# POOL makes the low parts of the weights in pieces of 256 columns in place of 512

## The chip, the cores and the metric

The kernel runs on one core of one Trainium2 chip. The time is the device time of one execution in microseconds (us). The engines are named as the profile names them: PE (matrix multiplications), PEld (its weight loads), ACT, DVE and POOL (elementwise work), SP (issues transfers). Each engine runs its own instruction stream, and the streams wait for each other by semaphores.

## The reference

Two transformer-like layers over x of 512 tokens by 1024 features, all in float32. Layer 0 mixes by a gated linear recurrence (4 heads) beside a differential attention (4 heads), layer 1 by an attention with forget gates (16 heads); each layer ends in a SwiGLU block.

```python
def reference(x, even_w_in, even_w_out, ..., fox_w_in, fox_w_out, ..., ffn_w1, ffn_w2, ln1_g, ln1_b, ln2_g, ln2_b):
    for l in range(DEPTH):          # DEPTH = 2, D_MODEL = 1024, SEQ = 512, D_FF = 2816
        j = l // 2
        if l % 2 == 0:
            h = _even_mixer(x, even_w_in[j], even_w_out[j], lb_all[j], ..., l)
        else:
            h = _odd_mixer(x, fox_w_in[j], fox_w_out[j], fox_b_f[j], fox_qnorm_g[j], fox_knorm_g[j])
        x = _layer_norm(ALPHA * x + h, ln1_g[l], ln1_b[l])
        x = _layer_norm(ALPHA * x + _swiglu(x, ffn_w1[l], ffn_w2[l]), ln2_g[l], ln2_b[l])
    return x
```

Nearly all the arithmetic is products of x (or of an activation of the same height) with the weight matrices.

## The kernel before

**Split products.** Each float32 operand of a large product is split into a high part in PE's own format (fp32r) and a low part, the remainder. A product is then three matmuls, `high x low`, `low x high`, `high x high` (function `products`, lines 507 to 509), summed in a PSUM bank.

**Chunks of weights.** All weights are cut into 107 chunks in the order of use, nearly all of 2048 columns on 128 partitions (four have 1024, one has 128). A chunk passes four stations:

- SP loads it into `w_raw`, a ring of two (`load`, L1021). Before it loads chunk c it waits until the low part of chunk c-2 is made (`lo_ready`).
- ACT rounds it into `w_hi`, a ring of three, in one operation (`hi_upto`, L1118), at places in ACT's stream that are written out by hand. It waits for the load and for PE to be done with chunk c-3.
- POOL subtracts: `w_lo = w_raw - w_hi`, a ring of three (L1078), four operations of 512 columns a chunk. Only the last one reports (`lo_ready`). This is all that POOL does.
- PE waits for both parts (`weights_in`) before the first product with the chunk.

In the forgetting attention, POOL's operations of some chunks are each put behind a step of DVE (`lo_behind`: the operation waits for `qn_done`, the normalised queries and keys of one token tile, L1709), so that it runs in a stretch that DVE leaves free. The table has one entry for each 512 columns.

**Stages in order.** Input projections and the recurrence of layer 0 (0 to 190 us: PE alternates between pieces of projections and products of the recurrence, L811 to L834, while DVE scales `qT`, `kT`, `spans`, L1498 to L1501, and normalises heads, `refine`, L1440 to L1443, L1562); differential attention (190 to 285); output projection and layer norm (285 to 330; `norm`, L1633 to L1655, then `split_lo`, L1425); SwiGLU (330 to 690), layer norm; forgetting attention (695 to 997); output projection, layer norm, SwiGLU, layer norm (to 1401). In a layer norm, tile t of x passes through a fixed chain on DVE: L1633 adds the product to the residual, L1634 and L1641 take statistics, ACT forms a root, L1645 subtracts the mean and multiplies by the gain, L1648 to L1650 refine the root, L1655 scales and adds the bias. PE then turns the tile (L578), and ACT and DVE split it again.

The order of the instructions on each engine is fixed in the program. Nothing is planned at run time.

Of the kernel before, what the change touches and what calls it, by code (L numbers as in the profile page):

```python
# [128 lines left out]
def build(nc, w, out):  # L129
    chunks = weight_chunks(w)  # L130
    stage_chunks = {}
    for c, (stage, _, _) in enumerate(chunks):
        stage_chunks.setdefault(stage, []).append(c)

    with ExitStack() as ctx:
# [188 lines left out]
        n = 0  # L324
# [81 lines left out]
        for i, (piece, _) in enumerate(fox_steps):  # L406
            if piece:
                c, p = piece
                if c == chunk_at("foxk0") and p % 2 == 0:
                    round_at[i] = c + 1 + p // 2  # L410
                elif c != chunk_at("foxk0") and p == (3 if chunks[c][0] == "foxv0" else 1):
                    round_at[i] = c + 2
# [7 lines left out]
        def nth(kinds, u):  # L420

            return sum(1 for k, _, _ in units[:u] if k in kinds)
# [644 lines left out]
        @block.gpsimd  # L1067
        def _(pool):
            for c, (_, _, size) in enumerate(chunks):
                pool.wait_ge(hi_ready, c + 1)  # L1070
                if c >= RING:
                    pool.wait_ge(*chunk_used[c - RING])
                for a in range(0, size, 512):
                    n = min(512, size - a)
                    behind = lo_behind.get(c, [None] * 4)[a // 512]
                    if behind:
                        pool.wait_ge(S["qn_done"], behind)
                    ins = nc.gpsimd.tensor_tensor(w_lo[c % RING][:, a:a + n], w_raw[c % RAW][:, a:a + n],  # L1078
                                                  w_hi[c % RING][:, a:a + n].bitcast(F32), ALU.subtract)
                ins.then_inc(lo_ready, 1)  # L1080
# [780 lines left out]
```

## Time and profile before

| | |
|---|---|
| time, median of 3 runs | 1402.65 us (1400.98 to 1405.59) |
| the profiled execution's own time | 1402.81 us |
| its span, first to last instruction | 1401.0 us |
| PE busy | 1348.9 us, 96% |
| DVE busy | 474.6 us, 34% |
| ACT busy | 495.6 us, 35% |
| POOL busy | 531.5 us, 38%, 417 operations of L1078 |
| mean granted clock of PE | 0.989 of 2.4 GHz |

The span is the profiler's view of the execution. 1.8 us of the device time lie outside it. Ends of PE's matmuls are modelled and overlap, so that their spacing, not their duration, tells what one costs.

### The profile page before, as it was taken

The page shows a single profiled execution, that of the slowest core. Times are in us where ns is not written, and L with a number is a line of the kernel's source. Part 1 is how long each engine was busy: PE and PEld are TensorE (multiplying, and loading weights), DVE is VectorE, ACT ScalarE, POOL GpSimd, SP SyncE. Part 2 cuts the span into 40 slices and gives each one's busy share as a digit, 9 for nine tenths or more (in the row PEclk, how much of TensorE's full clock was granted, in tenths as well). Part 3 has the DMA queues.
Part 4 walks back from the last instruction along what each step waited for, and adds up shares of the span by engine and source line. Part 5 has one row for each costly group of instructions (what it writes and reads, how often), then busy time and mean ns, then how long its engine had stood idle before and what let it go on. Part 6 is the DMA issues. An engine that isn't in the chain of part 4 may idle for free.

```text
span 1401.0 us, 18949 instructions
## 1 busy us (share of the span) xinstructions
PE 1348.9 (96%) x7304; PEld 1125.0 (80%) x7304; DVE 474.6 (34%) x956; ACT 495.6 (35%) x824; POOL 531.5 (38%) x421
## 2 busy tenths in 40 slices
PE   7998999698999999999999999999999999999997
PEld 7887877588888888888788888877788888888886
DVE  3365435556111111010634555644561111110005
ACT  4313155523322232211255665654333222232111
POOL 5514041232444445544234312222434444445440
PEclk9999999799999999999999999999999999999999
DMA  6311021113333332333133222211223333323221
GB/s 213 110 61 61 31 92 60 61 33 89 91 91 90 104 107 76 120 97 127 25 96 94 66 62 61 61 61 61 91 85 96 90 90 95 108 84 120 91 105 60
DMA packets 141400, 119.60 MB, mean 85 GB/s; under 512 B 5664, under 2 KB 120576, under 8 KB 141312
## 3 DMA queue, kind: packets, MB, share of 16 engines
q1 hardware_dynamic: 141072, 118.10, 27.0%
q8 instruction: 58, 0.95, 0.3%
q10 hardware_dynamic: 240, 0.31, 0.1%
q14 instruction: 30, 0.25, 0.1%
HBM read 116.20 MB, written 2.10 MB: 84 GB/s over the span
## 4 chain that ended last, share of the span: by engine, by line
PE 83%; DVE 7%; ACT 4%; issue 4%; POOL 1%; DMA 0%; ACTq 0%; DVEq 0%; SPq 0%; POOLq 0%
PE banks L507 25%; PE banks L508 25%; PE banks L509 25%; ACT w_hi L1118 1%; PE banks L816 1%; PE banks L974 1%; PE banks L940 1%; PE banks L956 1%; POOL w_lo L1078 1%; PE banks L834 1%; DVE small L1602 1%; DVE xT_lo L1425 1%; PE banks L880 1%; DMA w_raw<-in_even_w_in_dram 0%; DVE x_res L1645 0%
## 5 line engine op out<-in xcount | busy, mean ns | idle before, releaser
L1078 POOL TENSOR_TENSOR w_lo<-w_raw,w_hi 128x512 fp32r<-128x512 f32 x417 | 531.3, 1304 | 838.1 <-ACT w_hi L1118 782.6
L507 PE MATMUL banks<-xT_lo,w_hi 128*128 128x512 f32 (+2 forms) x1024 | 384.3, 375 | 2.5 <-DVEq L1426 2.4
L509 PE MATMUL banks<-xT_hi,w_hi 128*128 128x512 f32 (+2 forms) x1024 | 380.5, 372 | 0.0
L508 PE MATMUL banks<-xT_hi,w_lo 128*128 128x512 f32 (+2 forms) x1024 | 380.4, 372 | 0.0
L1118 ACT ACTIVATE w_hi<-w_raw 128x2048 fp32r<-128x2048 f32 (+1 forms) x107 | 200.0, 1869 | 194.5 <-PE banks L509 151.4
L507 PEld LDWEIGHTS banks<-xT_lo,w_hi 128*128 128x128 f32 (+1 forms) x1024 | 192.2, 188 | 37.4 <-issue 5.1
L509 PEld LDWEIGHTS banks<-xT_hi,w_hi 128*128 128x128 f32 (+1 forms) x1024 | 192.1, 188 | 33.6
L508 PEld LDWEIGHTS banks<-xT_hi,w_lo 128*128 128x128 f32 (+1 forms) x1024 | 192.2, 188 | 32.6
L1675 DVE TENSOR_TENSOR banks<-silu_g,banks 128x512 f32<-128x512 f32 x44 | 30.6, 696 | 403.1 <-PE banks L509 403.1
L507 PE MATMUL banks<-w_lo,xT_hi 128*128 128x256 f32 (+1 forms) x480 | 159.0, 331 | 5.1 <-POOL w_lo L1078 2.8
L508 PE MATMUL banks<-w_hi,xT_lo 128*128 128x256 f32 (+1 forms) x480 | 153.9, 321 | 0.0
L509 PE MATMUL banks<-w_hi,xT_hi 128*128 128x256 f32 (+1 forms) x480 | 153.8, 320 | 0.0
L507 PE MATMUL banks<-w_lo,hT_hi 128*128 128x512 f32 x352 | 137.1, 390 | 0.0
L509 PE MATMUL banks<-w_hi,hT_hi 128*128 128x512 f32 x352 | 137.0, 389 | 0.0
L508 PE MATMUL banks<-w_hi,hT_lo 128*128 128x512 f32 x352 | 136.9, 389 | 0.0
L1288 ACT ACTIVATE silu_g<-banks 128x512 f32<-128x512 f32 x44 | 26.3, 597 | 306.9 <-PE banks L509 306.9
L507 PEld LDWEIGHTS banks<-w_lo,xT_hi 128*128 128x128 f32 x480 | 92.1, 192 | 15.2 <-issue 6.5
L509 PEld LDWEIGHTS banks<-w_hi,xT_hi 128*128 128x128 f32 x480 | 92.2, 192 | 6.6
L508 PEld LDWEIGHTS banks<-w_hi,xT_lo 128*128 128x128 f32 x480 | 92.4, 192 | 5.9
L1633 DVE SCALAR_TENSOR_TENSOR x_res<-x_res,banks 128x512 f32<-128x512 f32 x32 | 22.0, 687 | 212.5 <-PE banks L509 211.8
L509 PEld LDWEIGHTS banks<-w_hi,hT_hi 128*128 128x128 f32 x352 | 66.1, 188 | 13.7
L507 PEld LDWEIGHTS banks<-w_lo,hT_hi 128*128 128x128 f32 x352 | 66.1, 188 | 13.7
(198 smaller groups left out, 1259.9 us busy)
## 6 DMA issues: line engine op xcount, KB each, us to landing
w_raw<-in_ffn_w_dram SPq DMA_DIRECT2D x92, 512.0 KB, 4.6
w_raw<-in_ffn_w_dram SPq DMA_DIRECT2D x20, 1024.0 KB, 4.9
w_raw<-in_fox_w_in_dram SPq DMA_DIRECT2D x16, 1024.0 KB, 5.8
w_raw<-in_even_w_in_dram SPq DMA_DIRECT2D x14, 1024.0 KB, 5.0
w_raw<-in_even_w_out_dram SPq DMA_DIRECT2D x4, 1024.0 KB, 5.1
w_raw<-in_fox_w_out_dram SPq DMA_DIRECT2D x4, 1024.0 KB, 5.0
x_res<-in_x_dram SPq DMA_DIRECT2D x4, 512.0 KB, 7.9
out_dram<-x_res SPq DMA_DIRECT2D x3, 512.0 KB, 2.6
```

The costliest lines, as they stand in the source:

```text
L507: mm(acc, l_hi, r_lo, start=first, stop=False)
L508: mm(acc, l_lo, r_hi, start=False, stop=False)
L509: return mm(acc, l_hi, r_hi, start=False, stop=final)
L816: ins = mm(halves(acc[:, tok], z)[:, :, 1, :], k[:, tok], halves(q[:, tok], z)[:, :, 1, :], start=True, stop=True)
L834: ins = mm(acc[:, t * P:(t + 1) * P], scT[:, h % 2, PAIR[(s, t)], :], iv[:, s, h * P:(h + 1) * P], start=s == 0, stop=s == t)
L880: mm(acc[:, 0:n], bqT[rows, h, i * P:(i + 1) * P], bkT[rows, h, 0:n], start=True, stop=False)
L940: mm(acc[:, 0:n], qk[rows, j % 2, 0, pair % 2, i * P:(i + 1) * P], qk[rows, j % 2, 1, pair % 2, 0:n], start=True, stop=False)
L1078: ins = nc.gpsimd.tensor_tensor(w_lo[c % RING][:, a:a + n], w_raw[c % RAW][:, a:a + n], w_hi[c % RING][:, a:a + n].bitcast(F32), ALU.subtract)
L1118: chain(fn(w_hi[c % RING][:, 0:size], w_raw[c % RAW][:, 0:size], ACT.Copy), hi_ready)
L1288: release(fn(silu_buf(j), acc[:, :], ACT.Silu), (f"up{l}", j, 0))
L1633: release(stt(xs, xs, ALPHA, full(key)[:, :], ALU.mult, ALU.add), key)
L1675: release(tt(h_buf(j), silu_buf(j), acc[:, :], ALU.mult), (f"up{l}", j, 1))
```

## The change

POOL's loop steps by 256 columns and not by 512. A chunk of 2048 columns takes eight operations in place of four, one of 1024 takes four in place of two, and the one of 128 columns stays one operation. The data, the ring buffers, the semaphore and the place where it is raised (after the last operation) are the same. The entry of `lo_behind` is still taken by 512 columns, so two operations in a row wait for the same value, of which the second wait is met at once.

```
--- before.py
+++ after.py
@@ -1070,8 +1070,8 @@
                 pool.wait_ge(hi_ready, c + 1)
                 if c >= RING:
                     pool.wait_ge(*chunk_used[c - RING])
-                for a in range(0, size, 512):
-                    n = min(512, size - a)
+                for a in range(0, size, 256):
+                    n = min(256, size - a)
                     behind = lo_behind.get(c, [None] * 4)[a // 512]
                     if behind:
                         pool.wait_ge(S["qn_done"], behind)
```

## Rows read from the trace of the kernel before

**Rows 1.** The page, part 1: busy time and share of each engine.

```profile
PE 1348.9 (96%) x7304; PEld 1125.0 (80%) x7304; DVE 474.6 (34%) x956; ACT 495.6 (35%) x824; POOL 531.5 (38%) x421
```

**Rows 2.** The waits: who waited for whom, us in total, times, longest.

```profile
POOL w_lo L1078 <- ACT w_hi L1118: 782.6, 103, 33.9
...
PE banks L816 <- DVE spans L1501: 7.0, 6, 3.3
PE banks L890 <- ACT pT_diff L1246: 4.3, 3, 2.1
...
PE banks L507 <- POOL w_lo L1078: 2.8, 2, 2.4
...
PE banks L507 <- issue: 2.2, 2, 1.8
```

**Rows 3.** The timeline of POOL in the first SwiGLU: start, duration, operation, idle before.

```profile
395.30 5.04 POOL L1078 TENSOR_TENSOR w_lo<-w_raw,w_hi 128x512 fp32r<-128x512 f32 x4 [5.84 <-ACT w_hi L1118]
```

**Rows 4.** The timelines of POOL and DVE at 310 and at 695 us.

```profile
310.06 2.34 POOL L1078 TENSOR_TENSOR w_lo<-w_raw,w_hi 128x512 fp32r<-128x512 f32 x1
309.96 1.29 DVE L1645 SCALAR_TENSOR_TENSOR x_res<-x_res,stats,rows_even 128x1024 f32<-128x1024 f32 x1
...
313.89 1.29 DVE L1655 SCALAR_TENSOR_TENSOR x_res<-x_res,stats,rows_even 128x1024 f32<-128x1024 f32 x1
...
696.42 1.44 POOL L1078 TENSOR_TENSOR w_lo<-w_raw,w_hi 128x128 fp32r<-128x128 f32 x1
695.19 2.36 DVE L1645 SCALAR_TENSOR_TENSOR x_res<-x_res,stats,rows_ffn 128x1024 f32<-128x1024 f32 x1
...
698.11 0.16 DVE L1650 SCALAR_TENSOR_TENSOR stats<-stats 128x1 f32<-128x1 f32 x1
```

**Rows 5.** The timeline of POOL at the start: its four smallest operations.

```profile
0.24 0.10 POOL L1850 MEMSET const-float32-0.0<- 128x1 f32 x1 [0.24 <-issue]
...
0.34 0.10 POOL L1850 MEMSET const-uint8-127<- 128x1 uint8 x1
```

**Rows 6.** The timelines of POOL, DVE and PE in the opening.

```profile
10.46 4.97 POOL L1078 TENSOR_TENSOR w_lo<-w_raw,w_hi 128x512 fp32r<-128x512 f32 x4 [10.02 <-ACT w_hi L1118]
14.77 0.69 DVE L1425 TENSOR_TENSOR xT_lo<-banks,xT_hi 128x512 fp32r<-128x512 f32 x1 [0.22 <-DVE xT_lo L1425]
15.53 0.36 PE L507 MATMUL banks<-xT_lo,w_hi 128*128 128x256 f32 x1 [0.63 <-DVEq L1426]
```

**Rows 7.** The timelines of POOL and PE where the forgetting attention starts.

```profile
691.49 6.37 POOL L1078 TENSOR_TENSOR w_lo<-w_raw,w_hi 128x512 fp32r<-128x512 f32 x5 [23.25 <-ACT w_hi L1118]
696.72 0.36 PE L507 MATMUL banks<-w_lo,xT_hi 128*128 128x256 f32 x1 [2.39 <-POOL w_lo L1078]
```

**Rows 8.** The timelines of POOL and PE at the second output projection.

```profile
997.71 10.02 POOL L1078 TENSOR_TENSOR w_lo<-w_raw,w_hi 128x512 fp32r<-128x512 f32 x8 [28.55 <-ACT w_hi L1118]
1007.88 0.47 PE L507 MATMUL banks<-w_lo,xT_hi 128*128 128x512 f32 x1 [0.45 <-POOL w_lo L1078]
1029.69 0.55 PE L578 MATMUL banks<-ident,x_res 128*128 128x128 f32 x3 [0.74 <-DVE x_res L1655]
```

**Rows 9.** The timelines of POOL and PE at two chunks of the forgetting attention.

```profile
716.72 1.26 POOL L1078 TENSOR_TENSOR w_lo<-w_raw,w_hi 128x512 fp32r<-128x512 f32 x1 [2.13 <-DVE qn L1709]
718.08 0.36 PE L507 MATMUL banks<-w_lo,xT_hi 128*128 128x256 f32 x1 [1.79 <-issue]
729.69 1.29 POOL L1078 TENSOR_TENSOR w_lo<-w_raw,w_hi 128x512 fp32r<-128x512 f32 x1 [0.95 <-DVE qn L1709]
731.08 0.47 PE L507 MATMUL banks<-w_lo,xT_hi 128*128 128x512 f32 x1 [0.39 <-issue]
```

**Rows 10.** The timelines of POOL, DVE and PE in the recurrence.

```profile
135.09 4.99 POOL L1078 TENSOR_TENSOR w_lo<-w_raw,w_hi 128x512 fp32r<-128x512 f32 x4 [4.50 <-ACT w_hi L1118]
136.42 1.22 DVE L1441 TENSOR_TENSOR stats<-stats 128x4 f32<-128x4 f32 x1
138.92 1.19 DVE L1443 TENSOR_TENSOR stats<-stats 128x4 f32<-128x4 f32 x1
140.14 1.25 DVE L1562 TENSOR_SCALAR o_even<-o_even,stats 128x128 f32<-128x128 f32 x4
142.47 0.74 PE L816 MATMUL banks<-qT,kT 128*128 128x64 f32 x5 [3.27 <-DVE spans L1501]
```

**Rows 11.** Windows: busy us (x instructions) of PE, PEld, DVE, ACT, POOL, then PE's clock.

```profile
697.00:701.00 4.00, 4.00 (x23) 4.00 (x22) 3.61 (x7) 0.04 (x1) 0.86 (x1) 0.57 0.84 226
701.00:706.00 5.00, 5.00 (x45) 4.80 (x45) 0.78 (x2) 1.20 (x2) 0.00 (x0) 1.00 0.64 242
```

More of the change, by code:

```diff
@@ L1072, in _ @@
                     pool.wait_ge(*chunk_used[c - RING])
-                for a in range(0, size, 512):
-                    n = min(512, size - a)
+                for a in range(0, size, 256):
+                    n = min(256, size - a)
                     behind = lo_behind.get(c, [None] * 4)[a // 512]
```

## The prediction

> **What bounds the kernel now.** The page's busy times come first: PE is busy 96% of the span, POOL 38% [rows 1]. PE sets the end, and POOL is no bound by its sum. The waits come second: POOL stood idle 782.6 us for ACT's high parts, and PE waited for POOL only twice, 2.8 us in all [rows 2]. In the SwiGLU stages, half the span, a chunk takes POOL 5.04 us and then it idles 5.84 us [rows 3]; a longer batch there disappears in that idle time. So the change can act in two ways only. It can delay the few chunks for whose low part PE stands waiting, or it can change how POOL and DVE get in each other's way. The third look was therefore at each of PE's idle gaps in the timeline, and at each operation of DVE that took longer beside POOL than its like did elsewhere.
>
> **POOL and DVE take turns.** At 309.96 DVE's L1645 and POOL's third operation start together. DVE takes its usual 1.29 us, to 311.25; POOL takes 2.34, to 312.40, 1.15 us after DVE [rows 4]. The other way round, L1441 and L1443 work on 4 columns and take 1.22 and 1.19 us [rows 10], where a DVE operation of that size with no POOL beside it takes 0.16 [rows 4]; each ends with the POOL operation that runs beside it. So a POOL operation and a DVE operation that reads two SBUF tensors exclude each other, and one that waits gets its turn when the other ends.
>
> **The price of one operation.** Two POOL operations of different width were held up by DVE: the 512 columns ended 1.15 us after it, the 128 columns at 697.86, 0.31 us after DVE's 697.55 [rows 4]. That is 0.84 us for 384 columns, 2.19 ns a column, or 1.12 us for 512 and 0.56 for 256. Four operations of 512 take 5.04 us, of which the last lasts 1.29, so they follow each other every 1.25 us [rows 3]. The rest, 1.25 - 1.12 = 0.13 us, is what an operation costs whatever its width. One of 256 then follows every 0.69 us, and a chunk takes 8 x 0.69 + 0.04 = 5.56 us for 5.04, 0.52 more. The fixed 0.13 us is the disputed number. From below, the smallest POOL operations follow each other every 0.03 us [rows 5]; from above, the whole 0.31 us of the 128 columns may be fixed [rows 4]. I take 0.13, because it follows from the very operation that is cut. In sum POOL gains 416 operations, 54 us, nearly all of it in its idle time.
>
> The Trainium skill (GPSIMD Engine Reference, section Elementwise, side-by-side cycle accounting) gives 2.6 cycles an element at 1.2 GHz for this operation, 2.17 ns, and 4497 ns for 2048 elements, which leaves 0.06 us fixed. The trace agrees on the slope. By the page's 0.06 the sum below would come to about +1.5 us.
>
> **Part by part, on PE's path.**
>
> *Opening.* POOL makes the first chunk's low part from 10.46 to 15.43; DVE's last needed split ends at 15.46; PE starts at 15.53 [rows 6]. Both are due together, so POOL's 0.52 us go onto the path: +0.5.
>
> *Start of the forgetting attention.* POOL works from 691.49; its fifth operation, which belongs to the next chunk, starts at 696.42, so the fourth ends at 696.46, and PE, idle since 694.33, starts at 696.72 [rows 7]. DVE's L1645 was issued at 695.19, just missed its turn, and ended at 697.55, 1.09 after POOL's last operation [rows 4]. With operations every 0.69 us, the sixth runs from 694.94 to 695.67 when L1645 is issued. L1645 gets the next turn, ends at 696.76, and two POOL operations are still to come: the first ends 0.31 + 128 x 0.00219 = 0.59 after it, the second 0.69 later, at 698.04. PE starts 1.6 us later, at 698.3. DVE gains nothing by it, since L1648 to L1650 now each wait for one of POOL's left operations. +1.6.
>
> *Second output projection.* Two chunks in a row, 8 operations, 10.02 us; PE waits 0.45 us for the end [rows 8]. Sixteen take 11.08: +1.06. PE later waits for DVE's layer norm by 0.74 us [rows 8], and that chain moves by somewhat less. +0.8.
>
> *Two chunks of the forgetting attention.* POOL's last quarter, put behind DVE's L1709, ends at 717.98 and 730.98, and PE starts 0.10 us after each; the waits call these 1.79 and 0.39 us "issue" [rows 2, 9]. Each quarter is now two operations: +0.13 twice, +0.3.
>
> *DVE's delays.* Where DVE runs several such operations in a row, halving POOL's does not halve the delay. After 136.1 POOL had three operations of 1.25 us to go, and L1441 to L1443 waited for one each; the four L1562 behind them then ran free in 1.25 us [rows 10]. Now six or seven of 0.69 us are to go: L1440 to L1443 wait some 0.5 us each, and three of the L1562 wait 0.4 to 0.5 each. Played through turn by turn, the row ends at 141.2 to 141.4 for 141.4 before. The chain at 309.96 ends at 315.18 (313.89 + 1.29) both times [rows 4]: L1645 and L1648 to L1655 wait for the four halves that the two whole ones were. What POOL still has to do when DVE arrives passes between DVE's operations in either cut. Only where DVE turns to PSUM or idles after one or two operations does something come back; I count -0.4 for the recurrence.
>
> Sum: 0.5 + 1.6 + 0.8 + 0.3 - 0.4 = +2.8 us. On the profiled execution, 1402.8, that is 1405.6; its own time lies 0.16 above the median, so against 1402.65 the forecast is 1405.4. The loads cost nothing: SP starts the next one 0.5 us later, and a chunk that is rounded every 10.9 us (5.04 + 5.84) hides it [rows 3]; without that cover it would be 0.5 us a chunk.
>
> **Rivals.**
>
> *DVE gets half its waits back (faster).* Nine of POOL's batches run shortly ahead of a gap of PE, and in each about two operations of DVE wait 1.05 us (1.22 - 0.17): 19 us. If short operations let DVE pass after half the time and no further waits came in, 9.5 would come back, less 3.2 of costs: 1396. For it speaks that each wait is a whole POOL operation long [rows 10]; against it the turn-by-turn count above, and that PE waits for ACT's copies (4.3 us, L1246) in the differential attention beside its 7.0 us for DVE's `spans` [rows 2]. It decides from some 7.4 us given back. The Trainium skill (SBUF — State Buffer, section Who interferes with whom) says that the one issued first holds the shared ports for the whole instruction and the other fully blocks; by that rule alone, shorter holds free DVE sooner. The trace agrees with the rule.
>
> *An operation costs more than 0.13 us fixed (slower).* 4 + 4 + 8 + 2 = 18 extra operations lie on PE's path. At the bound of 0.31 they cost 5.6 for 2.3 us: +6.1, 1408.8. It decides from about 0.21.
>
> *PE's clock (slower).* After the 2.4 us gap before 696.72 the granted clock fell: 0.57 on average from 697 to 701, 1.00 after [rows 11]; 23 matmuls ran in 4 us there against 45 in 5 us. A gap of 4 us may be followed by a longer stretch at 1.2 GHz, or a second place may fall. One such stretch costs 4 - 23/9 = 1.4 us; two more make +5.6, 1408.2.
>
> *No effect at all:* 1402.7, if the fixed cost is the 0.03 and DVE does not get in at 695.
>
> **How the numbers follow.** This measurement tells no change from one of 0.3%, 4.2 us. Forecast 0.60, inside that; no effect 0.05, inside; DVE's waits come back 0.08, of which 0.07 beyond; fixed cost 0.15 and clock 0.12, beyond. So faster 0.07, same 0.66, slower 0.27. The range reaches from 1401.5 (bound of 0.03, and a little given back) to 1410 (the two slower rivals, partly together). The forecast's own range is 1404 to 1406.8.
>
> **What would show it.** POOL: 833 operations of L1078, median near 0.73 us, 5.56 us for eight in the SwiGLU. PE's first L507 at 16.0; its gap at 694.3 near 4 us, with L1645 there at 1.57 us, not 2.36; its gap at 1007.4 near 1.5. The gap at 139.2 about as long as before. Eight operations in well over 5.8 us would make the fixed cost wrong; a gap at 694 that stayed at 2.9 would mean that DVE did not get in between; clearly shorter gaps of PE at 127 to 142 would show DVE's waits coming back.

## The result: 3.5 us slower, where 2.8 us was forecast

The kernel with 256 columns takes 1406.49 us (median of 14 runs, 1405.43 to 1408.77), the one before, beside it on the same chip, 1402.94 us (14 runs). The ratio is 1.0029, with a 95% interval of 1.002 to 1.0038. Against the 1402.65 us that the forecast was made on, +3.55 us is 1406.2; the forecast was 1405.4 with a range of 1401.5 to 1410. The profiled execution has a span of 1404.3 us for 1401.0, and a mean granted clock of 0.986 for 0.989.

Part 1 of the page after, and POOL's group (operations | busy us, mean ns of one | idle us, and for whom). They answer to [rows 1]:

```profile
PE 1351.9 (96%) x7304; PEld 1127.6 (80%) x7304; DVE 467.3 (33%) x956; ACT 496.3 (35%) x824; POOL 595.2 (42%) x837
...
L1078 POOL TENSOR_TENSOR w_lo<-w_raw,w_hi 128x256 fp32r<-128x256 f32 x833 | 595.0, 751 | 778.0 <-ACT w_hi L1118 727.0
```

POOL works 63.7 us more (54 were predicted), and its wait for ACT is 55.6 us shorter (782.6 in [rows 2]): the extra work lies in its idle time. DVE is busy for 7.3 us less, which is waiting that no longer sits inside its operations. PE is busy for 3.0 us more with the same 7304 matmuls; that goes with more time at the lower clock (worked out from the two traces: 42.5 us of the span at a granted clock of 0.50, before 33.4).

The timeline of POOL after, at the four places of [rows 6, 3, 7, 8]:

```profile
10.49 5.54 POOL L1078 TENSOR_TENSOR w_lo<-w_raw,w_hi 128x256 fp32r<-128x256 f32 x8 [10.05 <-ACT w_hi L1118]
...
395.84 5.61 POOL L1078 TENSOR_TENSOR w_lo<-w_raw,w_hi 128x256 fp32r<-128x256 f32 x8 [5.27 <-ACT w_hi L1118]
...
692.03 6.95 POOL L1078 TENSOR_TENSOR w_lo<-w_raw,w_hi 128x256 fp32r<-128x256 f32 x9 [22.98 <-ACT w_hi L1118]
...
999.76 11.16 POOL L1078 TENSOR_TENSOR w_lo<-w_raw,w_hi 128x256 fp32r<-128x256 f32 x16 [27.96 <-ACT w_hi L1118]
```

A chunk costs 5.54 to 5.61 us for a predicted 5.56, two in a row 11.16 for 11.08. In the SwiGLU the idle before it shrinks from 5.84 to 5.27 us and nothing else moves.

The timeline of PE after, where it waits (answers to [rows 6 to 9]):

```profile
16.13 0.36 PE L507 MATMUL banks<-xT_lo,w_hi 128*128 128x256 f32 x1 [0.98 <-POOL w_lo L1078]
...
698.82 0.55 PE L507 MATMUL banks<-w_lo,xT_hi 128*128 128x256 f32 x1 [3.95 <-POOL w_lo L1078]
...
720.10 0.35 PE L507 MATMUL banks<-w_lo,xT_hi 128*128 128x256 f32 x1 [1.94 <-issue]
...
733.25 0.47 PE L507 MATMUL banks<-w_lo,xT_hi 128*128 128x512 f32 x1 [0.56 <-issue]
...
1011.07 0.47 PE L507 MATMUL banks<-w_lo,xT_hi 128*128 128x512 f32 x1 [1.61 <-POOL w_lo L1078]
...
1032.92 1.09 PE L578 MATMUL banks<-ident,x_res 128*128 128x128 f32 x8 [0.75 <-DVE x_res L1655]
```

The wait of 2.39 us became 3.95, those of 1.79, 0.39 and 0.45 us became 1.94, 0.56 and 1.61. The last row is the later wait for DVE's layer norm: 0.75 for 0.74 us, so nothing of the longer wait at 1007 us is given back there.

PE issues the same matmuls in the same order in both kernels, so the start of the same matmul can be compared. Worked out from the two traces, us:

```
PE's matmul no.        32     500    724    760    1250   1650   3330   3560   5490   5600   7300
start before           15.53  98.24  142.47 150.15 242.74 338.09 702.37 733.00 1003.2 1027.9 1392.2
after minus before     +0.59  +0.37  +0.64  -1.33  -1.50  +0.54  +1.87  +2.17  +2.04  +3.21  +3.31
```

From 338 us on, every step of more than 0.15 us in this row is one of the predicted waits. Before 338 us the kernel gains 2 us at 144 and loses them again between 250 and 335. That is what the forecast did not have, and what half of the experiments are about.

### The profile page after: what moved, and what is told of

It is laid out like the page before. It is cut to its first block, busy times and chain, and to the rows that moved or that the text cites. A ratio compares the mean times of both kernels' runs of the same rounds, so it can differ in the third digit from the quotient of the medians.

```text
span 1404.3 us, 19365 instructions
## 1 busy us (share of the span) xinstructions
PE 1351.9 (96%) x7304; PEld 1127.6 (80%) x7304; DVE 467.3 (33%) x956; ACT 496.3 (35%) x824; POOL 595.2 (42%) x837
## 4 chain that ended last, share of the span: by engine, by line
PE 84%; DVE 6%; ACT 4%; issue 4%; POOL 2%; DMA 0%; ACTq 0%; DVEq 0%; SPq 0%; POOLq 0%
PE banks L507 25%; PE banks L509 25%; PE banks L508 25%; POOL w_lo L1078 2%; PE banks L816 2%; ACT w_hi L1118 1%; PE banks L974 1%; PE banks L940 1%; PE banks L956 1%; PE banks L834 1%; PE banks L578 1%; PE banks L880 1%; DMA w_raw<-in_even_w_in_dram 0%; DVE x_res L1645 0%; DVE small L1602 0%
## 5 line engine op out<-in xcount | busy, mean ns | idle before, releaser
L1078 POOL TENSOR_TENSOR w_lo<-w_raw,w_hi 128x256 fp32r<-128x256 f32 x833 | 595.0, 751 | 778.0 <-ACT w_hi L1118 727.0
L508 PEld LDWEIGHTS banks<-w_hi,hT_lo 128*128 128x128 f32 x352 | 66.1, 188 | 13.6
```

Source lines behind the costliest of these rows:

```text
L508: mm(acc, l_lo, r_hi, start=False, stop=False)
```

## Where the clock was low

The granted clock is 1.00 at 2.4 GHz and 0.50 at 1.2 GHz. The windows of PE before and after (busy us and number of instructions of PE, PEld, DVE, ACT, POOL; then PE's granted clock, DMA share, GB/s), first of the kernel before:

```profile
135.09:141.92 6.83, 3.86 (x20) 3.07 (x20) 6.37 (x12) 0.00 (x0) 4.99 (x4) 1.00 0.09 20
144.26:147.67 3.41, 3.41 (x13) 2.97 (x12) 2.65 (x9) 0.00 (x0) 0.00 (x0) 0.50 0.06 17
```

and of the kernel after:

```profile
135.09:141.92 6.83, 4.77 (x15) 4.19 (x16) 6.37 (x13) 0.00 (x0) 5.25 (x8) 0.50 0.16 45
144.11:147.67 3.56, 3.43 (x20) 3.02 (x20) 3.02 (x9) 0.00 (x0) 0.00 (x0) 1.00 0.15 50
...
698.29:701.71 3.42, 2.89 (x13) 2.92 (x14) 3.10 (x5) 0.00 (x0) 0.69 (x2) 0.50 0.53 114
```

Before, PE ran at 1.2 GHz from 144.26 us, when it was busy without a gap: 13 matmuls in 3.41 us, where after it does 20 in 3.56. After, it runs at 1.2 GHz from 135.09 to 141.92 us. In that stretch it would have waited for DVE's `spans` anyway, 3.27 us before 142.47 [rows 10]. Twice as long at the lower clock cost nothing that was left at matmul 732, and once at the wrong moment cost 1.6 us (matmuls 732 to 760).

The timelines of PE and DVE after, in this stretch, and behind them one row of DVE before (they answer to [rows 10]):

```profile
133.76 1.08 PE L816 MATMUL banks<-qT,kT 128*128 128x64 f32 x8 [2.22 <-DVE spans L1501]
137.15 1.94 PE L816 MATMUL banks<-qT,kT 128*128 128x64 f32 x8 [2.31 <-DVE spans L1501]
...
143.11 2.21 PE L816 MATMUL banks<-qT,kT 128*128 128x64 f32 x16
...
134.53 0.87 DVE L1498 TENSOR_TENSOR qT<-qT,spans 128x256 f32<-128x256 f32 x1
135.33 0.94 DVE L1499 TENSOR_TENSOR kT<-kT,spans 128x256 f32<-128x256 f32 x1
136.19 0.81 DVE L1501 TENSOR_TENSOR spans<-spans 128x128 f32<-128x128 f32 x1
...
137.91 0.38 DVE L1440 TENSOR_TENSOR stats<-stats 128x4 f32<-128x4 f32 x1
138.33 0.65 DVE L1441 TENSOR_TENSOR stats<-stats 128x4 f32<-128x4 f32 x1
139.01 0.66 DVE L1442 TENSOR_SCALAR stats<-stats 128x4 f32<-128x4 f32 x1
139.71 0.65 DVE L1443 TENSOR_TENSOR stats<-stats 128x4 f32<-128x4 f32 x1
...
141.69 0.42 DVE L1498 TENSOR_TENSOR qT<-qT,spans 128x256 f32<-128x256 f32 x1
```

```profile
141.43 0.43 DVE L1498 TENSOR_TENSOR qT<-qT,spans 128x256 f32<-128x256 f32 x1
```

Each DVE wait is halved (0.65 - 0.17 = 0.48 us for 1.05), and there are twice as many: POOL's batch starts at 134.40 and not at 135.09, and L1498 to L1501 wait 0.44, 0.52 and 0.53 us beside the three at L1441 to L1443. With L1440 that is 3.15 us of waiting for 3.23 before. DVE starts the L1498 behind its row 0.26 us later than before (141.69 for 141.43); it had started the L1498 ahead of the row 0.30 us later (134.53 for 134.23). So DVE's chain is as long as it was, to 0.04 us.

PE has no gap at matmul 724 any more, since the matmuls ahead of it are slow enough to fill it. It starts this matmul at 143.11 us, 0.64 later than before and 0.38 later than `spans` would have let it (ready at 142.58, and before at 142.32 for a start at 142.47). Eight matmuls on it waits for DVE's next `spans` again, 0.13 us, and is 0.26 us late. What is gained comes afterwards, from the clock: 1.6 us up to matmul 760.

## The experiments

Theory A is the forecast's: the cost stands at six chunks (first of all, `foxq0`, `foxk0`, `foxv0`, and the two of the second output projection), and is POOL's time there plus one turn lost to DVE. The rivals stand beside it in each expectation. The widths are set at the two changed lines; `piece` is the number of columns of one operation, and `chunk_at` gives a chunk's number. "Beside" names the kernel before as it ran on the same chip. Its median differs from one such series to the next (1402.14 to 1404.5 us), so that ratios are compared and not times. A trace shows one execution of a kernel, and a kernel with one run has no interval.

**1 and 2. The six chunks alone at 512, and alone at 256.**

```diff
-                for a in range(0, size, 256):
-                    n = min(256, size - a)
+                for a in range(0, size, piece := 512 if c in CRITICAL else 256):    # kernel 1
+                for a in range(0, size, piece := 256 if c in CRITICAL else 512):    # kernel 2
+                    n = min(piece, size - a)
```

`CRITICAL` stands for the numbers of `a_f` 0, `foxq0`, `foxk0`, `foxv0` 0 and `out1` 2 and 3.

> Pieces of 256 everywhere, but of 512 in the six chunks for whose low part PE stood waiting (the first of a_f, foxq0, foxk0, the first of foxv0, the last two of out1). Theory A (the time is lost at those six chunks, by the fixed cost of the extra operations and by DVE's turn at 695): PE's gaps there are those of the kernel before (0.6, 2.4, 1.8, 0.4 and 0.5 us) and the time is back at 1402 to 1403.5. Theory B (the loss is spread over the other 101 chunks, by port traffic, semaphores or the clock): no more than 1 us comes back, 1405.5 to 1406.5.

> The complement: pieces of 256 in those six chunks alone, 512 elsewhere. Theory A: the whole loss is here, +3.5 to +4 us, 1406.5 to 1407. Theory B: within 1 us of the kernel before, 1403 to 1404.

Measured, kernel 1: 1401.36 us (12 runs) beside 1402.14, ratio 0.9993 (0.9983 to 1.0003). The timeline of PE in kernel 1 has the waits of before again:

```profile
16.02 0.35 PE L507 MATMUL banks<-xT_lo,w_hi 128*128 128x256 f32 x1 [0.49 <-POOL w_lo L1078]
...
697.03 0.36 PE L507 MATMUL banks<-w_lo,xT_hi 128*128 128x256 f32 x1 [2.40 <-POOL w_lo L1078]
...
1009.94 0.47 PE L507 MATMUL banks<-w_lo,xT_hi 128*128 128x512 f32 x1 [0.47 <-POOL w_lo L1078]
```

101 of the 107 chunks are in pieces of 256 here and six in pieces of 512, and the loss is gone. So it lies in the six, as Theory A has it, and the other 392 of the 416 added operations cost nothing on the whole. The profiled execution was the slowest of the twelve, 1404.96 us: a stretch at 0.50 from 718.47 us, which neither kernel has, made it 1.5 us later between matmuls 3330 and 3560.

Measured, kernel 2: 1411.74 us (6 runs, 1405.48 to 1413.42) beside 1402.14, ratio 1.006 (1.004 to 1.008). That is more than Theory A's 3.5 to 4 us. PE's waits are those of the kernel after (3.95, 1.94, 0.56 and 1.65 us). The rest goes with the clock; windows of kernel 2:

```profile
145.16:151.99 6.83, 6.77 (x20) 5.74 (x21) 2.98 (x9) 0.00 (x0) 0.00 (x0) 0.50 0.07 22
701.53:708.36 6.83, 6.04 (x28) 6.07 (x29) 3.59 (x5) 0.00 (x0) 0.94 (x2) 0.50 0.78 241
```

Both stretches are 6.83 us where before has 3.41, and in both PE is busy nearly all the time; two that neither kernel has stand at 15.46 and 725.43 us. Of its six runs two had a mean clock of 0.987 and took 1405.5 and 1406.9 us, four had 0.982 or 0.983 and took 1411.2 to 1413.4. The first pair is near Theory A's time; the other four are some 6 us longer in one and the same program. The profiled execution is one of them. It ends 9.4 us behind the one before, of which its longer waits for POOL are 3.7 us, and most of the rest stands at the four stretches named.

**3. DVE lets POOL finish first** (on the kernel after).

```diff
                     xs = x_res[:, t, :]
+                    if tag == "n2_0" and t == NT - 1:
+                        dve.wait_ge(lo_ready, chunk_at("foxq0") + 1)
                     step(stt(xs, xs, st[:, 12:13], gain, ALU.subtract, ALU.mult))
```

> The changed kernel, with one wait more: before L1645 of the last tile of the layer norm ahead of the forgetting attention, DVE waits for the low part of foxq0. Turn theory (of the 1.6 us lost at 694, 1.04 are DVE's turn between two of POOL's operations and 0.52 are their fixed cost): PE's gap at 694.9 shrinks from 3.95 to 2.9 us, and L1645 runs 1.29 us. Pace theory (POOL is that slow by itself): the gap stays at 3.9 us. The span is 1 us shorter or the same; only the profile can tell.

Measured: 1404.55 us (one run), span 1402.7. The timelines of PE and DVE in kernel 3 (L1645 stands at L1647 here):

```profile
697.03 0.43 PE L507 MATMUL banks<-w_lo,xT_hi 128*128 128x256 f32 x1 [2.96 <-ACT xT_hi L1130]
...
696.91 1.35 DVE L1647 SCALAR_TENSOR_TENSOR x_res<-x_res,stats,rows_ffn 128x1024 f32<-128x1024 f32 x1 [2.02 <-POOL w_lo L1078]
```

PE's wait is 2.96 us, where 2.9 was expected, for 3.95. The profile puts it down to ACT, whose `xT_hi` was ready at 696.77 us; POOL's eighth operation ended at the same 696.77, and PE starts 0.26 us after that, as it starts 0.25 us after POOL in both kernels. So 1.0 of the 1.56 us is the one turn that DVE gets between two operations of POOL, and the other 0.57 is POOL's own longer batch.

**4. Pieces of 128 columns everywhere.**

```diff
-                for a in range(0, size, 256):
+                for a in range(0, size, 128):
```

> Pieces of 128 everywhere, sixteen to a chunk. Fixed-cost theory: an operation follows every 0.28 + 0.13 = 0.41 us, a chunk takes 6.6 us (5.04 at 512, 5.56 at 256); PE starts at 17.1, its gap at 694 is near 5 us and that at 1007 near 3.5 us; the time 1409 to 1410. If the cost of a piece shrinks with its width, the chunk takes 5.6 us and the time stays at 1406.5.

Measured: 1410.42 us (4 runs) beside 1402.14, ratio 1.0059 (1.0044 to 1.0075). Timelines of POOL and PE in kernel 4:

```profile
403.88 6.76 POOL L1078 TENSOR_TENSOR w_lo<-w_raw,w_hi 128x128 fp32r<-128x128 f32 x16 [4.12 <-ACT w_hi L1118]
...
1001.59 13.42 POOL L1078 TENSOR_TENSOR w_lo<-w_raw,w_hi 128x128 fp32r<-128x128 f32 x32 [26.81 <-ACT w_hi L1118]
...
698.10 0.55 PE L507 MATMUL banks<-w_lo,xT_hi 128*128 128x256 f32 x1 [6.06 <-DVEq L1426]
...
1015.15 0.77 PE L507 MATMUL banks<-w_lo,xT_hi 128*128 128x512 f32 x1 [3.65 <-POOL w_lo L1078]
```

A chunk is 6.76 us long (6.6 was expected). With 5.04 and 5.61 us for the wider pieces, each added operation costs 0.14 us: (5.61 - 5.04) / 4 and (6.76 - 5.61) / 8. The wait at 1007 us came as expected (3.5), the one at 694 us is 6.06 for about 5, because DVE got two long turns in the batch, for L1645 and for L1655 (two of POOL's operations took 1.43 us for 0.45). The time is right. In the recurrence this kernel did something that the turn count forbids: from matmul 500 to 732, where PE waits for DVE, it took 43.73 us for 45.74. At 128 columns DVE does get time back. (It started this stretch 2.4 us late, behind the opening's longer wait and a stretch at 0.50 from 18.02 us.)

**5. Where does the early gain come from? 256 columns for the chunks of layer 0's mixer only.**

```diff
-                for a in range(0, size, 256):
+                for a in range(0, size, piece := 256 if 0 < c < chunk_at("out0") else 512):
```

> Pieces of 256 only in the chunks between the first one and the first output projection (recurrence and differential attention, 23 chunks), 512 elsewhere. Theory T (turns: what POOL still has to do passes between DVE's operations in either cut): PE's point of 144.8 us moves by -0.3 to -0.5, and what comes before 282 beyond that is the granted clock falling at other moments; time within 0.2% of the kernel before. Theory G (DVE's waits do come back here): PE is 2 us early at 250 and stays so; 1400 to 1401.

Measured: 1401.33 us (12 runs) beside 1404.29, ratio 0.9983 (0.9974 to 0.9993). That is a gain that can be told from nothing, though it lies within the 0.2% that the turn theory allowed. From matmul 500 to 732 PE took 45.85 us for 45.74, but it did not wait for DVE at matmul 732; DVE itself had its `spans` ready 45.48 us after matmul 500, for 45.60 before. So DVE's part is shorter by 0.1 us alone, as the turn count says. By matmul 760 it is 1.5 us ahead of where it stood at matmul 500. Its window of low clock:

```profile
135.42:142.25 6.83, 5.90 (x18) 5.06 (x19) 6.33 (x15) 0.00 (x0) 4.11 (x6) 0.50 0.21 66
```

It stands where the kernel after has it, before DVE's `spans` are ready. PE is 2.1 us ahead at matmul 1250 and stays so, as the rival had it, but not by DVE: the turns held, and the gain comes by the clock.

**6. Does the clock need the waits? The kernel after, with 15 idle matmuls at 694 us.** They multiply parts of `hT_hi` and `hT_lo` into a PSUM bank that is free there; what they compute is added work that nothing reads.

```diff
+                def fill(n, w, x):
+                    who, count = last[acc_bank[1][0]]
+                    pe.wait_ge(freed[who][acc_bank[1][0]], count)
+                    for _ in range(n):
+                        mm(psum[acc_bank[1][0]][:, :], w[:, 0, 0:P], x[:, 0, :], start=True, stop=True)
...
+                    if tag == "n2_0":
+                        fill(15, hT_hi[:, 12:13, :], hT_lo[:, 12:13, :])
                     early(0)
```

> The changed kernel, with 15 matmuls of 512 columns more on PE, into a bank that nobody reads, in its gap at 694.9 (3.3 us of work in 3.95 us of waiting). It adds to the computation and changes no result. Clock theory: the granted clock doesn't fall after the gap, and the products after 698.8 that run at 1.2 GHz for 3.4 us run at 2.4: 1.4 to 1.7 us less, 1404.8 to 1405. If the fall has nothing to do with PE's idle time, or the half-speed stretch costs nothing: 1406.5.

Measured: 1403.91 us (10 runs) beside 1404.29, ratio 1.000 (0.9991 to 1.001). The timeline of PE in kernel 6 and, in a fence of its own, a window (columns as above):

```profile
698.23 0.36 PE L507 MATMUL banks<-w_lo,xT_hi 128*128 128x256 f32 x1 [0.60 <-POOL w_lo L1090]
```

```profile
697.00:701.00 4.00, 3.40 (x26) 2.99 (x25) 3.65 (x6) 0.00 (x0) 1.35 (x3) 1.00 0.43 87
```

The wait for POOL is as late as ever, but PE is busy for most of it, and the granted clock stays at 1.00 where the kernel after had 0.50 from 698.29 to 701.71. Only at 1397 us, in the last layer norm, does it fall again. The ratio went from 1.0029 to 1.000 with no change to POOL or DVE. That is some 4 us, where 1.4 to 1.7 were expected. The traces place 1.2 of it here: from matmul 3290 to 3330 the kernel after loses 1.33 us against the kernel before, this one 0.13. Where the rest comes from is not shown; the profiled executions differ by 1.9 us in all.

**7. The same on the kernel before:** 9 idle matmuls at 694 us, 13 at 323.6, 3 at 327.9.

```diff
+                        if tag == "n1_0" and t == NT - 2:
+                            fill(13, o_hi_e, o_lo_e)
                         turn(t)
+                    if tag == "n1_0":
+                        fill(3, o_hi_e, o_lo_e)
+                    if tag == "n2_0":
+                        fill(9, hT_hi[:, 12:13, :], hT_lo[:, 12:13, :])
                     early(0)
```

> The kernel before (512), with such idle matmuls in three gaps of PE: 9 at 694.3, 13 at 323.6, 3 at 327.9. It adds to the computation and changes no result. Clock theory: no fall of the clock at 328.6 and 697.2, where 3.4 us each ran at half speed: 2.8 to 3.4 us less, 1399 to 1400, faster than both kernels. Otherwise: no change, 1402.5.

Measured: 1402.12 us (12 runs) beside 1404.29, ratio 0.9983 (0.9974 to 0.9991). The granted clock is 1.00 from 283.32 to 1396.07 us; the stretches at 328.58 and 697.22 us are gone. Each saved about what was expected of it: against the kernel before, PE gains 1.4 us from matmul 1500 to 1600, and 1.4 from 3290 to 3330. In this execution it had lost 1.8 us up to matmul 760, behind stretches at 0.50 from 129.72 and 143.38 us, so that the end comes only 0.6 us earlier.

**8. Only `foxq0` at 256.**

```diff
-                for a in range(0, size, 256):
+                for a in range(0, size, piece := 256 if c == chunk_at("foxq0") else 512):
```

> Pieces of 256 in the chunk foxq0 alone. Turn theory: all that changes is PE's gap at 694.3, from 2.4 to 3.95 us, 0.52 of it by fixed cost and 1.04 by DVE's turn; L1645 there takes 1.57 us and not 2.36. From there on PE is 1.6 us late, less what a clock that is low in idle time doesn't cost. Pace theory: the gap grows by 0.5 only, and L1645 stays near 2.4.

Measured: 1407.12 us (one run), span 1405.3. The timeline of PE in kernel 8 and, in a fence of its own, a window:

```profile
698.46 0.55 PE L507 MATMUL banks<-w_lo,xT_hi 128*128 128x256 f32 x1 [3.94 <-POOL w_lo L1078]
```

```profile
697.44:704.27 6.83, 5.81 (x27) 5.84 (x28) 3.79 (x6) 0.00 (x0) 1.18 (x3) 0.50 0.73 228
```

The wait is that of the kernel after to 0.01 us, and matmul 3296 behind it is 1.74 us late. But the low clock behind it lasts 6.83 us and not 3.42, and a further 3.41 us stand at 721.34: at the end it is 4.3 us late. The same wait of 3.95 us cost 1.3 us in one execution and 4.1 in the other (4.28 - 0.19, by matmuls 3290 and 3560).

**9. One operation of 2048 columns for the late chunks, no idle matmuls; 256 in layer 0's mixer.**

```diff
-                for a in range(0, size, 256):
+                for a in range(0, size, piece := 2048 if c in (chunk_at("foxq0"), chunk_at("out1", 2), chunk_at("out1", 3)) else 256 if 0 < c < chunk_at("out0") else 512):
```

> The same widths without idle matmuls. Fixed-cost theory: an operation of 2048 takes 4.5 to 4.6 us for the 5.04 of four; PE's gap at 694 is 1.9 and not 2.4 us, that at 1007 is gone; with the recurrence's -2.4: 1400 to 1401. If a long operation has no less overhead: gaps of 2.4 and 0.45, 1401.3 as with the recurrence alone.

Measured: 1401.53 us (12 runs) beside 1404.5, ratio 0.9981 (0.997 to 0.9991). Timelines of POOL, PE and DVE in kernel 9:

```profile
689.77 5.96 POOL L1078 TENSOR_TENSOR w_lo<-w_raw,w_hi 128x2048 fp32r<-128x2048 f32 x2 [23.25 <-ACT w_hi L1118]
...
694.58 0.35 PE L507 MATMUL banks<-w_lo,xT_hi 128*128 128x256 f32 x1 [1.97 <-POOL w_lo L1078]
...
693.47 1.94 DVE L1645 SCALAR_TENSOR_TENSOR x_res<-x_res,stats,rows_ffn 128x1024 f32<-128x1024 f32 x1
695.44 0.30 DVE L1648 SCALAR_TENSOR_TENSOR stats<-stats 128x1 f32<-128x1 f32 x1
```

PE waits 1.97 us (2.39 before) and not at all at 1007 us. L1645 waits behind the whole operation, and none of PE's gaps that follow is put down to it. Both waits are as the fixed cost has them, but the time cannot tell it: the ratio is all but that of kernel 5 (0.9983), where these chunks had 512. The two chunks ahead of the second output projection take POOL:

```profile
995.59 9.19 POOL L1078 TENSOR_TENSOR w_lo<-w_raw,w_hi 128x2048 fp32r<-128x2048 f32 x2 [28.54 <-ACT w_hi L1118]
```

In 2, 8, 16 and 32 operations they take 9.19, 10.02, 11.16 and 13.42 us (this kernel, before, after, kernel 4): 0.14 us for each added operation at every step.

**10. The same widths with idle matmuls** (at the places of kernel 7, whose `fill` it has).

```diff
-                        fill(9, hT_hi[:, 12:13, :], hT_lo[:, 12:13, :])
+                        fill(8, hT_hi[:, 12:13, :], hT_lo[:, 12:13, :])
```

> All that helped so far: pieces of 256 in the recurrence and the differential attention, one operation of 2048 for foxq0 and the last two chunks of out1, 512 elsewhere, and idle matmuls in PE's gaps at 694 (8), 323 (13) and 328 (3), which add to the computation and change no result. If the parts add up: -2.4 (recurrence), -2.4 (clock) and -0.9 (0.4 us of fixed cost at 694, 0.5 at 1007): 1397 to 1398. If the clock's gain and the recurrence's are the same one: 1399.5 to 1400.5.

Measured: 1398.0 us (6 runs, 1396.73 to 1399.95) beside 1404.5, ratio 0.9958 (0.9943 to 0.9974). The parts add up, as the first expectation has it. This version beats both kernels; the medians are 6.5 us apart from the one before, the ratio makes it 5.9 (3.7 to 8.0).

**11. 1024 columns in layer 0's mixer.**

```diff
-                for a in range(0, size, 256):
+                for a in range(0, size, piece := 1024 if 0 < c < chunk_at("out0") else 512):
```

> Pieces of 1024 in the chunks of recurrence and differential attention, 512 elsewhere. Turn theory: from 98.2 to 144.0 PE needs 45.7 us as with 512 and 256 (45.6 to 45.9), give or take 0.5, and the time depends on when the clock falls: 1402 to 1405. If short pieces let DVE through sooner, long ones hold it: 47 us or more, and 1404 to 1406.

Measured: 1409.81 us (8 runs) beside 1404.5, ratio 1.0045 (1.003 to 1.0059). Timelines of POOL, DVE and PE in kernel 11:

```profile
124.71 4.85 POOL L1078 TENSOR_TENSOR w_lo<-w_raw,w_hi 128x1024 fp32r<-128x1024 f32 x2 [15.59 <-ACT w_hi L1118]
...
124.38 0.43 DVE L1498 TENSOR_TENSOR qT<-qT,fT 128x256 f32<-128x256 f32 x1
124.80 2.56 DVE L1499 TENSOR_TENSOR kT<-kT,fT 128x256 f32<-128x256 f32 x1
127.28 2.56 DVE L1501 TENSOR_TENSOR spans<-fT 128x256 f32<-128x256 f32 x1
...
129.98 1.94 PE L816 MATMUL banks<-qT,kT 128*128 128x64 f32 x8 [3.18 <-DVE spans L1501]
```

Two DVE operations of 0.42 us take 2.56 each, one beside each half of the chunk. Matmuls 500 to 732 take 47.54 us. So this stretch takes 47.54, 45.74, 45.63 and 43.73 us with 1024, 512, 256 and 128 columns. From 512 to 256 the turn count holds to 0.1 us; it is not a law for all widths. Here its expectation (45.7 us) failed, and that of its rival (47 us or more) came true; the time lies above both.

**12. One operation for the first and the late chunks, 512 elsewhere.**

```diff
-                for a in range(0, size, 256):
+                for a in range(0, size, piece := 2048 if c in (chunk_at("a_f"), chunk_at("foxq0"), chunk_at("out1", 2), chunk_at("out1", 3)) else 512):
```

> One operation of 2048 for the first chunk, foxq0 and the last two of out1, 512 elsewhere. Fixed-cost theory: the first chunk's low part is there after 4.5 us, 0.5 before DVE's split, so PE waits for DVE alone; gaps of 1.9 us at 694 and none at 1007. L1645 at 695 waits for the one long operation in any case. Otherwise the gaps are those of the kernel before.

Measured: 1399.77 us (one run), span 1398.0. The waits at 694 and 1007 us are those of kernel 9. The half-speed stretch of kernel 12 in the recurrence stood at 135.56 to 138.97 us, although the pieces there have the 512 columns of before. PE's wait before `spans` shrank from 3.27 to 1.62 us with it, and the kernel was 1.9 us ahead at 150 us. At the start PE still waited for POOL (1.18 us), and not for DVE alone as expected. What one operation saves in the opening stays open: from one execution to the next, PE's first matmul starts up to 1 us earlier or later with the arrival of x, and the kernel ran once.

## Why the prediction was right, and where not

**Price of an operation: right.** 0.14 us fixed for the forecast's 0.13, now from five widths, 2048 to 128 columns (1024 in the last section). The rival with 0.21 or more is out. By the estimate of 0.06 us from the figures of the Trainium skill (GPSIMD Engine Reference, section Elementwise, side-by-side cycle accounting) a chunk in eight pieces would have taken some 5.3 us (5.04 + 4 x 0.06); the runs show 5.54 to 5.61, and here the measurement decides.

**Opening: right.** +0.59 for +0.5; PE waits for POOL, no longer for DVE. Of this 0.37 is left at matmul 500.

**Start of the forgetting attention: right, with its mechanism.** The timeline of DVE after, at 695 us (answers to [rows 4]):

```profile
695.74 1.56 DVE L1645 SCALAR_TENSOR_TENSOR x_res<-x_res,stats,rows_ffn 128x1024 f32<-128x1024 f32 x1
697.34 0.56 DVE L1648 SCALAR_TENSOR_TENSOR stats<-stats 128x1 f32<-128x1 f32 x1
697.93 0.65 DVE L1649 SCALAR_TENSOR_TENSOR stats<-stats 128x1 f32<-128x1 f32 x1
698.62 0.38 DVE L1650 SCALAR_TENSOR_TENSOR stats<-stats 128x1 f32<-128x1 f32 x1
```

L1645 takes 1.56 us for a predicted 1.57 and 2.36 before, then the three small ones wait for one operation of POOL each. PE's wait grew by 1.56 us, predicted 1.6; kernel 3 took away exactly the turn. The matmuls behind moved by only 1.33 us, because the 3.42 us of low clock now lie partly in the wait (PE busy for 2.89 of them, before for 3.41).

**Two chunks of the forgetting attention: right.** +0.15 and +0.17 for 0.13 each.

**Second output projection: the discount was wrong.** PE's wait grew by 1.16 us, POOL's batch by 1.14. I let 0.26 of 1.06 come back in the layer norm. Its wait for DVE stayed at 0.75, and the matmuls behind moved by 1.17.

**DVE's delays in the recurrence: right to 0.3 us as a sum of turns, and wrong as to what the time would do.** Counted -0.4, measured -0.04 over DVE's row from 134 to 142 us, and -0.11 over matmuls 500 to 732. The count had the waits at L1440 to L1443 and at three of the L1562; they fell on L1498 to L1501 and L1441 to L1443, because POOL's batch began 0.7 us earlier, and their sum hardly changed (3.15 us for 3.23). "The gap at 139.2 about as long as before" was wrong: it went, since slower matmuls filled it, and gaps of 2.22 and 2.31 us stood ahead of it in place of 1.02, 1.23 and 0.80. The step that failed is that shifts of the waits add up to shifts of the end. At the granted clock they did not: -1.6 us at 144 to 148, then +1.6 between 250 and 290 us (half-speed from 261.39 for 6.83 us, before from 263.73 for 3.41) and +0.44 at 330. They nearly cancelled in the profiled execution (+0.59 at 15.5 us, +0.54 at 338), so the sum of the other terms, 1.33 + 0.30 + 1.17, makes up the rest of the +3.3. That the forecast of +2.8 came so near owes something to this luck.

**The rivals.** "DVE gets half its waits back" was wrong in size: DVE's busy time shows 7.3 us less waiting, and PE received 0.1 of it in the recurrence, for as many new waits came in. It is right at 128 columns. The Trainium skill (SBUF — State Buffer, section Who interferes with whom) calls the ports that DVE and POOL share an exclusive lock, held by whoever issues first; kernel 11's 2.56 us for a DVE operation of 0.42 beside pieces of 1024 agrees. "PE's clock" was a minor mechanism of the forecast and is the larger part of what varies: kernels 6 and 7 gain 0.3 and 0.2% with PE kept busy, of which the traces place 1.2 us and twice 1.4 at the idle matmuls; and kernels 2 and 8 lose more to it than to their longer waits.

**Open:** why the clock falls at 135 us in one execution and at 144 in another. The traces show a pattern. In all eight profiled kernels with 256 or 128 columns in layer 0's mixer (after, 1, 3, 4, 5, 6, 9, 10) the low stretch begins between 133.96 and 137.49 us and is over by 144.20, and matmuls 732 to 760 take 1.6 us less than before in each. Of the five with 512, the kernel before and 2, 7 and 8 have it later, with its end between 147.67 and 151.99; only kernel 12 has it at 135.56 to 138.97. With 256 columns PE's gaps just ahead are longer (2.22 us, then 1.5 to 2.3) than with 512 (1.2 and 0.8 in all but kernel 7), which may be what brings the fall forward; with 128 they are 1.53 and 1.07. So the width matters, but it does not decide alone, and no run here separates it from the rest. Over many runs kernels 5 and 9 gain 0.17 and 0.19%. Kernel 2 shows two outcomes of one program.

## What to carry to other kernels

Before cutting a batch of one engine into more instructions, look for the few batches that somebody waits for: the fixed cost of an instruction counts there alone, and so do the turns that an engine sharing the SBUF gets at each new boundary. A long instruction protects a batch that is due, and a short one lets the other engine pass; set the width by place, not for all. When a wait of the matmul engine can't be removed, cheap matmuls in it may bring back much of what it costs (kernel 6: 1.2 us for the 1.56 by which the wait had grown), and shifts of a few microseconds should be judged over many runs, with the granted clock beside each.

## What was not expected of the hardware

- One program took 1405.5 us at a mean granted clock of 0.987 and 1413.4 at 0.982 (kernel 2). The kernel before scattered from 1400.0 to 1406.3 us over 21 runs.
- With 15 matmuls that compute nothing of use, in a wait of 3.9 us, the kernel was 0.3% faster (kernel 6, 1.0029 to 1.000).
- The fixed cost of a POOL operation in a row was the same 0.14 us from 2048 columns down to 128. The chunk of kernel 11 at 124.71 us, 4.85 us long in two pieces, has a turn of DVE in it; one that DVE leaves alone takes 4.73 us for 5.03 in four pieces (at 51.79 us before), 0.15 for each added operation. The timeline of POOL in kernel 11:

```profile
51.37 4.73 POOL L1078 TENSOR_TENSOR w_lo<-w_raw,w_hi 128x1024 fp32r<-128x1024 f32 x2 [5.80 <-ACT w_hi L1118]
```
